# A slot's row search with bfloat16 zero-one matrix and table on one Trainium2 core

## What is computed

```
logits = xt @ w_router + b_router
top_vals, top_idx = lax.top_k(logits, TOP_K)          # 4 of 32
gates = jax.nn.softmax(top_vals, axis=-1)
...
slot_tok = zeros.at[dest].set(flat_tok[order])        # rows sorted by expert, padded to 128
slot_gate = zeros.at[dest].set(flat_gate[order])
...
def expert_block(args):                               # one block of 128 rows, one expert
    xb, e = args
    hgu = xb @ w_up_gate[e] + b_up_gate[e]
    ...
    return hact @ w_down[e] + b_down[e]
ys = lax.map(expert_block, (xs, block_e))
return zeros.at[slot_tok].add(ys * slot_gate)
```

## Time and profile before

| what | value |
|---|---|
| median of 3 runs | 2566.66 us (2564.89 to 2574.68) |
| the profiled execution's own time | 2565.02 us |
| its span, first to last instruction | 2563.2 us |
| TensorE busy | 2368.1 us, 92% |
| VectorE busy | 1780.3 us, 69% |
| ScalarE busy | 1334.2 us, 52% |
| granted TensorE clock, mean | 0.95 of 2.4 GHz |
| bytes moved by DMA | 570.40 MB |

### The profile page before, as it was taken

How to read it: one execution, slowest core, us unless ns; L and a number is a source line. 1 busy time by engine, 2 the same in 40 slices (tenths; PEclk the granted TensorE clock), 3 DMA queues, 4 the chain that set the end, 5 groups by cost and what they waited for, 6 DMA issues and landing times.

```text
span 2563.2 us, 31147 instructions
## 1 busy us (share of the span) xinstructions
PE 2368.1 (92%) x10716; PEld 1867.0 (73%) x10716; DVE 1780.3 (69%) x2142; ACT 1334.2 (52%) x1520; POOL 149.5 (6%) x103
## 2 busy tenths in 40 slices
PE   5999988999998998677799999999999999999967
PEld 4865566888787885555577777877777787777756
DVE  7526645555624667564688888889888888988863
ACT  4353343333413236204467766776776677677643
POOL 1000000000000000001001110110111011011100
PEclk8989898999999999777799999999999999999998
DMA  8213303332121310216799999999999999999960
GB/s 312 87 66 106 141 1 99 99 99 95 41 78 66 113 66 1 91 48 230 256 357 368 360 361 369 365 361 366 367 361 362 367 365 357 370 368 360 364 227 33
DMA packets 286442, 570.40 MB, mean 223 GB/s; under 512 B 10500, under 2 KB 34983, under 8 KB 286343
## 3 DMA queue, kind: packets, MB, share of 16 engines
q1 hardware_dynamic: 273607, 523.69, 56.6%
q0 software_dynamic: 12768, 45.81, 6.5%
HBM read 542.70 MB, written 26.75 MB: 222 GB/s over the span
## 4 chain that ended last, share of the span: by engine, by line
PE 85%; DVE 7%; ACT 3%; issue 2%; DMA 1%; SPq 1%; DVEq 0%; POOL 0%; ACTq 0%; POOLq 0%
PE bank L1633 13%; PE bank L1635 13%; PE bank L1634 13%; PE bank L1303 6%; PE bank L1305 6%; PE bank L1304 6%; PE bank L1627 4%; PE bank L1284 4%; PE bank L1492 3%; PE bank L1493 3%; PE bank L1494 3%; PE bank L1622 2%; PE bank L1381 2%; PE bank L1363 1%; PE bank L1609 1%
## 5 line engine op out<-in xcount | busy, mean ns | idle before, releaser
L2211 DVE TENSOR_TENSOR w_lo<-stage,w_hi 128x2048 fp32r<-128x2048 f32 x364 | 818.6, 2285 | 73.2 <-ACT w_hi L1200 72.6
L1200 ACT ACTIVATE w_hi<-stage 128x2048 fp32r<-128x2048 f32 x364 | 685.5, 1912 | 228.2 <-PE bank L1635 223.9
L1633 PE MATMUL bank<-w_hi,xeT_hi 128*128 128x512 f32 x1056 | 439.3, 416 | 0.0
L1635 PE MATMUL bank<-w_hi,xeT_lo 128*128 128x512 f32 x1056 | 412.9, 391 | 0.0
L1634 PE MATMUL bank<-w_lo,xeT_hi 128*128 128x512 f32 x1056 | 412.6, 391 | 0.0
L1635 PEld LDWEIGHTS bank<-w_hi,xeT_lo 128*128 128x128 f32 x1056 | 199.0, 188 | 43.0
L1634 PEld LDWEIGHTS bank<-w_lo,xeT_hi 128*128 128x128 f32 x1056 | 199.7, 189 | 40.4
L1633 PEld LDWEIGHTS bank<-w_hi,xeT_hi 128*128 128x128 f32 x1056 | 200.5, 190 | 37.2
L1760 DVE TENSOR_TENSOR ring_low<-ring,half_top 128x2048 fp32r<-128x2048 f32 (+2 forms) x42 | 93.1, 2221 | 161.9 <-ACT half_top L943 161.6
L1305 PE MATMUL bank<-half_top,hT_low 128*128 128x512 f32 (+1 forms) x480 | 188.7, 393 | 0.0
L1633 PE MATMUL bank<-w_hi,eaT_hi 128*128 128x512 f32 x400 | 176.0, 440 | 0.0
(11 more groups left out here) (414 smaller groups left out, 3860.3 us busy)
## 6 DMA issues: line engine op xcount, KB each, us to landing
stage<-in_w_up_gate SPq DMA_DIRECT2D x264, 1024.0 KB, 7.5
stage<-in_w_down SPq DMA_DIRECT2D x132, 1024.0 KB, 5.1
ring<-in_w_ada SPq DMA_DIRECT2D x12, 2048.0 KB, 8.2
ring<-in_w_up SPq DMA_DIRECT2D x22, 1024.0 KB, 7.7
ring<-in_w_in SPq DMA_DIRECT2D x10, 2048.0 KB, 7.8
ring<-in_w_out SPq DMA_DIRECT2D x4, 2048.0 KB, 13.2
ring<-in_w_down SPq DMA_DIRECT2D x4, 2048.0 KB, 8.0
stage<-in_w_ple_gate SPq DMA_DIRECT2D x4, 1024.0 KB, 7.2
```

The costliest lines, as they stand in the source:

```text
L1200: fn(w_hi[top_of(h)][:, :], src[:, :], ACT.Copy).then_inc(s_hi, 1)
L1633: mm(bank[b][:, :], hi[:, kk, :], wh[:, k, :], start=False, stop=False)
L1635: ins = mm(bank[b][:, :], lo[:, kk, :], wh[:, k, :], start=False, stop=kk == KT - 1)
L2211: tt(w_lo[h][:, :], stage[h][:, :], w_hi[top_of(h)][:, :].bitcast(FP), ALU.subtract).then_inc(s_lo, 1)
```

## The change

`pick` becomes a bfloat16 tile of the same shape. The table becomes `found3`, bfloat16, 99 columns for each token tile: the token number in two parts (256 times the tile pair, and the rest, up to 255), a one, and each gate in three bfloat16 parts that sum to it exactly. The four products of `find` have 99 columns of bfloat16 instead of 34 of float32. The copy to `picked` takes 99 columns. The row number is made from three columns instead of two, in as many instructions, and the gate is a sum over three instead of a copy. The gates are first summed in `gate_of` (float32) and split behind the point at which the rank products are released. The constants table gets five more columns.

```diff
-               ("slots", ...), ("tok", p[:, None] + P * np.arange(NT)[None, :]),
-               ("trash", TRASH + p[:, None]), ("pmod", ...)]),
+               ("slots", ...), ("tok_low", p[:, None] + P * (np.arange(NT) % 2)[None, :]),
+               ("tok_high", np.tile(2 * P * (np.arange(NT) // 2), (P, 1))),
+               ("trash", TRASH + p[:, None]), ("no_trash", -(TRASH + p[:, None])), ("pmod", ...)]),
...
-    pick = at(R + 80 * KB, [P, NT, P], name="pick")
+    pick = at(R + 80 * KB, [P, NT, P], BF, name="pick")
+    found3 = at(R + 81 * KB, [P, NT, 3 + 3 * NE], BF, name="found3")
...
-    route = take_T([P, NT, 2 + NE], name="route")
+    gate_of = take_T([P, NT, NE], name="gate_of")
...
-    picked = take_T([P, 2 + NE], name="picked")
+    picked = take_T([P, 3 + 3 * NE], name="picked")
...
-                    ins = mm(bank[7][:, 0:2 + NE], pick[:, t, :], route[:, t, :], start=t == 0, stop=t == NT - 1)
+                    ins = mm(bank[7][:, 0:3 + 3 * NE], pick[:, t, :], found3[:, t, :], start=t == 0, stop=t == NT - 1)
...
-            link(ve.tensor_copy(route[:, :, 0], cc("tok")))
-            link(ve.memset(route[:, :, 1], 1.0))
+            link(ve.tensor_copy(found3[:, :, 0], cc("tok_high")))
+            link(ve.tensor_copy(found3[:, :, 1], cc("tok_low")))
+            link(ve.memset(found3[:, :, 2], 1.0))
...
-                    link(tt(route[:, :, 2:], eq[:, :, :], gk, ALU.mult))
+                    link(tt(gate_of[:, :, :], eq[:, :, :], gk, ALU.mult))
...
-                    link(tt(route[:, :, 2:], route[:, :, 2:], eqk[:, :, :], ALU.add))
+                    link(tt(gate_of[:, :, :], gate_of[:, :, :], eqk[:, :, :], ALU.add))
             link(ve.memset(ones[:, :], 1.0))
             dve.nop().then_inc(s_route, 1)
+            parts3 = [found3[:, :, 3 + k * NE:3 + (k + 1) * NE] for k in range(3)]
+            for k in range(3):
+                link(ve.tensor_copy(parts3[k], gate_of[:, :, :]))
+                if k < 2:
+                    link(tt(gate_of[:, :, :], gate_of[:, :, :], parts3[k], ALU.subtract))
...
-                ve.tensor_copy(picked[:, :], bank[7][:, 0:2 + NE]).then_inc(bank_taken[7], 1)
+                ve.tensor_copy(picked[:, :], bank[7][:, 0:3 + 3 * NE]).then_inc(bank_taken[7], 1)
...
-                ts(idx_f[:, 0:1], picked[:, 1:2], -1.0, 1.0, ALU.mult, ALU.add).then_inc(s_empty, 1)
+                stt(idx_f[:, 0:1], picked[:, 2:3], cc("no_trash"), picked[:, 1:2], ALU.mult, ALU.add).then_inc(s_empty, 1)
                 dve.wait_ge(s_empty, i + 1)
-                stt(idx_f[:, 1:2], idx_f[:, 0:1], cc("trash"), picked[:, 0:1], ALU.mult, ALU.add).then_inc(s_row, 1)
-                ve.tensor_copy(gates[:, slot_at(i)], picked[:, bass.ds(e + 2, 1)]).then_inc(s_gate, 1)
+                ts(idx_f[:, 1:2], idx_f[:, 0:1], picked[:, 0:1], cc("trash"), ALU.add, ALU.add).then_inc(s_row, 1)
+                three_parts = picked[:, 3:].rearrange("p (k e) -> p e k", k=3)
+                ve.reduce_sum(gates[:, slot_at(i)], three_parts[:, bass.ds(e, 1), :], axis=AX).then_inc(s_gate, 1)
```

More of the change, by code:

```diff
@@ L73, in constants @@
         ("c", [("tri", (p[:, None] <= p[None, :]) * 1.0), ("iota", np.tile(np.arange(S), (P, 1))),
-               ("slots", np.tile(np.arange(MAXSLOT), (P, 1))), ("tok", p[:, None] + P * np.arange(NT)[None, :]),
-               ("trash", TRASH + p[:, None]), ("pmod", np.tile((p % 32)[:, None], (1, P)))]),
+               ("slots", np.tile(np.arange(MAXSLOT), (P, 1))), ("tok_low", p[:, None] + P * (np.arange(NT) % 2)[None, :]),
+               ("tok_high", np.tile(2 * P * (np.arange(NT) // 2), (P, 1))),
+               ("trash", TRASH + p[:, None]), ("no_trash", -(TRASH + p[:, None])), ("pmod", np.tile((p % 32)[:, None], (1, P)))]),
     ]
```

## The result

The changed kernel took 2547.35 us in the median of five runs (2541.95 to 2550.84), the kernel before 2566.66. The ratio is 0.9912, 95% interval 0.9893 to 0.9932: 0.9% less, 19.3 us by the medians. A second set of five runs gave 0.9916 (0.9902 to 0.993). The prediction was 2545.2. Its forecast held 2541 to 2552 with a chance of 0.74; with rival 1 it gave 0.86 to 2540 to 2555, and 0.87 to faster by more than 0.5%.

A forecast was written before the change was run, and what follows sets the result against it. TensorE's instructions laid end to end were taken to bound the kernel. 20.1 us from searches plus 1.35 ahead of the loop made 21.4 saved, so 2545.2 us; range 2541 to 2552, chance 0.74.

The forecast's parts named there:

- rival 1: Search in the loop: a bfloat16 pair takes 81 ns as load and product overlap less; 17.5 us saved, 2549; chance 0.12.
- What bounds: Loop over slots: TensorE, busy 37.40 of 37.40 us, sets the period; whatever is taken out of its instructions shortens it.
- The search: Four bfloat16 products of 99 columns at 0.05 us a pair: 0.20 us for a search instead of 0.81, 0.61 saved.
- In the loop: 32 searches in the loop plus that of slot 2, each 0.61 us shorter, all on TensorE's path: 20.1 us.
- Ahead of the loop: Before the loop, partly at 1.2 GHz: -0.69 and -1.0 for searches 0 and 1, +0.24 cast, +0.1 copy and sum: -1.35 us.
- Covers: Ahead of the loop: splitting the gates, 1.6 us, lies in VectorE's 6.35 us wait for the rank products and costs nothing.
- slack at bank 7: In the loop, between VectorE's copy freeing bank 7 and the next transposes: shrinks from 1.57 to 0.89 us, worst case 0.20.
- Rival 3: VectorE is late at bank 7, needing 0.96 us more work before the copy than counted; about 2556 us; chance 0.04.
- rival 2: DMA loads hold the loop's period at 37.43 us, leaving mainly the terms before the loop; about 2564 us; chance 0.05.
- a rate that no longer falls to zero: DMA rate at a period's end, 12 and 0 GB/s before: staying above zero was named as showing that DMA holds the period.
- rival 4: Searches: the type change puts load and product in series, 0.30 us a pair, 1.20 a search; slower, 2579 us; chance 0.03.
- rival 5: Narrow products still run as two passes at float32 speed; only terms before the loop move, within 2 us of 2566; chance 0.02.

The follow-up runs named there:

- second profile: The changed kernel unchanged, timed and profiled again beside a run with bfloat16 rank products on the same chip: 2546.13 us, ratio 0.9916 to the kernel before.

## Why the prediction was right

- **What bounds.** "The period is TensorE's own instructions laid end to end" held: +0.20 us of search gave +0.20 of period, three products fewer gave -0.13.
- **The search.** Forecast 0.20 us from the load's record of 97 ns and the price of a column; measured 0.20. The reason given stands too: 198 columns add the stream of 99 more, and 35 columns with the same load take 0.03 a pair, so columns and not the load set it. What I didn't foresee is the floor near 0.03 for narrow products. One premise was off without harm: I let the 34 float32 columns stream in 0.015 us, the price of a split product's column, where a float32 record takes nearly twice that, 0.029. Both are far under 0.101.
- **The Trainium skill's figure** of about 81 ns for a matmul of 128 columns in a stream with weight loads (TensorE: Matmul & The Clock Gate, "Back-to-back issue gap") doesn't hold here. 99 columns took 0.05 us a pair and 198 columns 0.09; at 0.43 ns for a column between them, 128 would take 0.063, an estimate. Rival 1, 0.081 for the pair of 99, falls.
- **In the loop.** Forecast 32 x 0.61 = 19.5 us; the stretch from slot 1 on is shorter by 19.11 in one profile and by 1216.72 - 1197.34 = 19.38 in the other. By the periods 32 x 0.62 = 19.8 are due, so 0.7 and 0.4 are missing. They go with the clock at the start of the stretch, where TensorE restarts after a hole of 6.8 us at the lower level. Products come 0.43 us apart until 1271.30 before and until 1277.74 after, that is for 4.5 us after the restart in one and 6.2 in the other; in the second profile it is 5.5 (1266.12 to 1271.65). Such products stand 0.43 us apart instead of 0.23, so 1.7 and 1.1 us more of them cost about 0.8 and 0.5, an estimate. The forecast had no term for this, and its 0.61 a search, for 0.62 in the period, hid a little of it. The chain of waits of the kernel before (start us, us, what):

```profile
1270.87 0.43 PE bank L1635
1271.30 0.36 PE bank L1633
1271.88 0.23 PE bank L1635
```

That of the changed kernel:

```profile
1277.31 0.43 PE bank L1635
1277.74 0.26 PE bank L1636
1278.00 0.23 PE bank L1637
```

- **Ahead of the loop.** Forecast -1.96 with the search of slot 2 (+0.24 to the release, then -2.2); measured +0.25 - 1.70 = -1.45, and in the second profile +0.25 - 2.15 = -1.90. From search 1 to the search of slot 2 the forecast was -1.0, with some of the gain given back because the clock need not rise sooner; measured 20.49 - 19.78 = 0.71, and 1.15 in the second profile. Both lie in the 0.7 to 1.3 that I gave. Search 1 itself fell from 1.73 us to 0.31 (1238.13 to the bias product at 1238.44), and products at the lower level took part of that back: they last until 1237.19 before and 1243.56 after, 3.4 and 5.1 us behind their bias product. The added 0.24 for the cast came out as said. The wait of 0.69 vanished, but less of it arrived than I had counted: from the first rank product to search 1 are 23.02 us before and 22.64 after, 0.38 less where 0.69 - 0.1 = 0.59 was forecast. The wider copy and the index instructions took 0.99 us up to the next instruction instead of 0.80, twice the 0.1 that I had put against it, and the copy of the rank products' bank came 0.07 later.
- **Covers.** The splits cost nothing where they stand and 1.4 us where they don't. The slack at bank 7 came out as 0.89 us, to the hundredth, but stood for the wrong instruction: the transposes that need bank 7 are the second four, 0.44 later. Rival 3 would have needed 1.4 us of added work, not 0.96.
- **DMA** (rival 2) didn't hold the period. By the same sum as before, 370 x 36.81 = 13.6 MB at 387 GB/s, it would hold it at 35.2 us, an estimate that no run tried. Its limit has come nearer: the lowest slice at the end of a period went from 0 to 117 GB/s. I had named a rate that no longer falls to zero as a sign of rival 2; it came, and the period fell all the same, so it was a sign of less slack and not of the rival.
- **Serial pairs** (rival 4) and **no effect** (rival 5) are excluded by the pairs of 0.05.
- **The total.** 2545.2 forecast, 2547.35 and 2546.13 measured. As a saving, 21.4 us were forecast; the medians give 19.3 in the first set and 2567.41 - 2546.13 = 21.28 in the second, the stretches behind the logits 20.4 and 21.3. That a median lies within 2 us of the forecast is in part luck, since one kernel's logits come up to 5 us apart; the stretches are the firmer test.

## What to carry to other kernels

A zero-one matrix is exact in bfloat16, and so is a float32 table split into three parts. As the stationary side of a narrow product it paid twice here: half as many records, and each half as far from the next (0.05 for 0.101 us), so look for narrow float32 products on TensorE's path before wide ones. Price such a product by the nanoseconds of a column, with the distance of starts and not the load's record as the measure (records of 104 ns stood 0.027 apart), and check who stands in front of the bank it frees: which of several transposes needs it is part of the slack. Where executions differ by more than the effect, cut the span at the same instructions in both traces and compare the stretches.

## What the runs showed of the hardware that I had not expected

- A bfloat16 pair of load and product with 35 columns starts every 0.03 us at the upper level of the clock (0.12 for four), and one with 32 columns every 0.027 at the lower level (14 from 1212.43 on within 0.4 us), with a stationary side of 128 columns each time.
- A float32 record of 99 columns took 0.109 us, the same as the transposes of 128 columns (0.87 for eight), and 0.101 with 34 columns; one of 512 columns took 0.43.
- VectorE writes 512 bfloat16 elements a row from float32 operands in the same 0.69 us as float32 ones.
- The same kernel's first 1200 us differed by 5.0 us between two profiled executions (1204.41 and 1199.39 at the logits).
